# A PEER feed-forward in one block: first products moved behind and between other work, one-hot rows on two engines

## The reference

```python
q = (hf @ w_q).reshape(T, PEER_HEADS, 2, PEER_HALF)
sc = jnp.einsum('thpd,hpkd->thpk', q, subkeys)
s1, i1 = lax.top_k(sc[:, :, 0], 16)
s2, i2 = lax.top_k(sc[:, :, 1], 16)
cand = s1[..., :, None] + s2[..., None, :]          # 16 x 16 pairs
top_s, pos = lax.top_k(cand, 16)                    # the 16 best of them
idx = i1 * 128 + i2 of these; gate = softmax(top_s)
act = gelu(einsum('chkd,cd->chk', u[idx], h))
out = einsum('chk,chkd->cd', gate * act, v[idx])
```

## Time and profile before

| | us |
|---|---|
| median of 3 runs | 3452.93 (3451.11 to 3649.39) |
| profiled execution, span | 3467.7 |
| norm of the feed-forward begins | 2036.7 |
| list of 155 steps | 2193.8 to 2904.3 |
| second products on TensorE | 2932.4 to 3458.8 |

### The profile page before, as it was taken

One profiled execution on the slowest core, in us unless ns is written; L12 is line 12 of the kernel. 1 busy time (PEld: TensorE's weight loads), 2 busy tenths in 40 slices (PEclk: granted clock), 3 DMA queues, 4 the chain that ended last, 5 costly groups with the idle time before them and its releaser, 6 DMA issues. The chain is left out here.

```text
span 3467.7 us, 33649 instructions
## 1 busy us (share of the span) xinstructions
PE 3066.9 (88%) x12681; PEld 2229.5 (64%) x12681; DVE 1723.3 (50%) x3505; ACT 1076.1 (31%) x1596; POOL 488.8 (14%) x357
## 2 busy tenths in 40 slices
PE   7887999699999598778979879698898986999998
PEld 3445666444444244564746568698898986888887
DVE  2255422200000205543442328787879797788886
ACT  2133421100000126674421222234434443333332
POOL 0000000111111000000000000003314143344442
PEclk9995999699999798889779989899999998999999
DMA  3110061488888210021002211357859688999996
GB/s 142 44 50 25 1 145 64 194 329 309 313 315 309 85 49 37 25 97 44 1 26 102 83 55 61 123 193 246 324 178 336 233 305 292 342 369 374 368 374 238
DMA packets 159776, 624.04 MB, mean 180 GB/s; under 512 B 12161, under 2 KB 84481, under 8 KB 128257
## 3 DMA queue, kind: packets, MB, share of 16 engines
q1 hardware_dynamic: 90496, 319.87, 26.1%
q0 software_dynamic: 50688, 276.85, 21.1%
q10 hardware_dynamic: 18432, 25.17, 2.0%
HBM read 555.76 MB, written 66.09 MB: 179 GB/s over the span
## 5 line engine op out<-in xcount | busy, mean ns | idle before, releaser
L1841 POOL DMA_INDIRECT RG<-in_un,EI x128 | 181.6, 1419 | 1400.0 <-DVE EI L2060 1105.3
L2275 PE MATMUL bank<-VH,GL 128*128 128x512 f32 x768 | 300.2, 391 | 29.9 <-DVE VR0r L2264 29.9
L2277 PE MATMUL bank<-VH,GH 128*128 128x512 f32 x768 | 299.7, 390 | 0.0
L1841 POOL DMA_INDIRECT RG<-in_vn,EI x128 | 216.5, 1691 | 446.7 <-DVE X L1855 429.9
L1133 PE MATMUL bank<-UP,HX 128*128 128x512 f32 x480 | 213.0, 597 | 9.4 <-DVE HX L1087 5.5
L1194 DVE SCALAR_TENSOR_TENSOR HN<-SLU,HR,bank 128x256 f32<-128x256 f32 x44 | 21.1, 481 | 344.2 <-ACT SLU L1168 344.2
L2275 PEld LDWEIGHTS bank<-VH,GL 128*128 128x128 f32 x768 | 144.8, 189 | 60.7 <-issue 30.4
L1855 DVE SCALAR_TENSOR_TENSOR X<-RG,DG,X 128x1024 f32<-128x1024 f32 x128 | 164.1, 1282 | 28.2 <-DMA RG<-in_vn,EI 24.1
L1825 PE MATMUL bank<-HTl,UH1r 128*128 128x384 f32 x512 | 174.5, 341 | 0.0
L1826 PE MATMUL bank<-HTh,UH1r 128*128 128x384 f32 x512 | 174.2, 340 | 0.0
L1825 PE MATMUL bank<-HTl,UH0r 128*128 128x384 f32 x512 | 173.3, 338 | 0.0
(11 more groups left out here) (518 smaller groups left out, 6569.3 us busy)
## 6 DMA issues: line engine op xcount, KB each, us to landing
UR<-in_u SPq DMA_DIRECT2D x64, 1024.0 KB, 5.5
VR<-in_vn SPq DMA_DIRECT2D x32, 2048.0 KB, 9.2
W<-in_weights SPq DMA_DIRECT2D x20, 1536.0 KB, 7.3
W<-in_weights SPq DMA_DIRECT2D x14, 2048.0 KB, 8.2
aspill<-GA ACTq DMA_DIRECT2D x128, 192.0 KB, 2.0
wspill<-VR SPq DMA_DIRECT2D x12, 2048.0 KB, 9.2
WW<-wspill SPq DMA_DIRECT2D x32, 768.0 KB, 13.9
AV<-aspill SPq DMA_DIRECT2D x32, 768.0 KB, 16.0
```

The costliest lines, as they stand in the source:

```text
L1841: e.indirect_dma_start(RG[q % RR], None, d["un" if what == "u" else "vn"][:, :], off).then_inc(*row_in[q % RR].up(16))
L2275: e.matmul(bk, r(gl[:, a, t]), r(vh[:, a, :]), start=g == 0 and a == 0, stop=False)
L2277: i = e.matmul(bk, r(gh[:, a, t]), r(vh[:, a, :]), start=False, stop=g == 31 and a == 3)
```

## The change

All of the feed-forward now stands in one block; the query weights have memory of their own, so that their loads and those of u are issued at the start. The search takes the splits of the first two u tiles along.

Of the 128 first products the list keeps 100: 0.95 in a step of choice (54 in 56 steps), 0.47 in another. Eight follow behind the last outer product, and 20 stand between second products, one behind each odd step of the first 40. 104 of the 256 gathered rows lie in the list, the others beside the second products.

Of four OB rows VectorE makes two. ScalarE makes the other two, each as Abs(iota − key) into AB and then Relu(gate − gate x AB), which is the gate at the key and 0 elsewhere. For that ScalarE writes −key and −gate into IN when it writes IA. The outer product waits for both.

A second step now takes all 1024 columns of two rows a (before: 512 columns of four), so v comes in 64 loads of 1 MB (three buffers) and a in 64 of 384 KB (three buffers). The low part of a lies in AV's own place; GL is gone. The last second step signals per token block, and the output leaves in four parts.

The diff, cut:

```diff
-                    for j in range(4):
-                        t = 4 * n + j
-                        i = e.tensor_scalar(OB[n % 2][:, j, :], cc("iota"), IA[:, 1, t:t + 1], IA[:, 2, t:t + 1], ALU.is_equal, ALU.mult)
-                    i.then_inc(*h_hot.up(1))
...
+            def dve_hot(e, n):
+
...
+                t4 = span(n, 4)
+                e.tensor_tensor(OA[n % 2], cc("iota").unsqueeze(1).to_broadcast([128, 4, 128]), IA[:, 0, t4].unsqueeze(2).to_broadcast([128, 4, 128]), ALU.is_equal)
+                for j in range(2):
+                    t = 4 * n + j
+                    i = e.tensor_scalar(OB[n % 2][:, j, :], cc("iota"), IA[:, 1, t:t + 1], IA[:, 2, t:t + 1], ALU.is_equal, ALU.mult)
+                i.then_inc(*h_hot.up(1))
...
+            def act_hot(e, n):
+
...
+                for j in (2, 3):
+                    t = 4 * n + j
+                    k = as_(e.activation(AB[n % 2][:, j - 2, :], cc("iota"), ACT.Abs, bias=IN[:, 0, t:t + 1]))
+                e.wait_ge(as_.sem, k)
+                for j in (2, 3):
+                    t = 4 * n + j
+                    i = e.activation(OB[n % 2][:, j, :], AB[n % 2][:, j - 2, :], ACT.Relu, bias=IA[:, 2, t:t + 1], scale=IN[:, 1, t:t + 1])
+                i.then_inc(*h_act.up(1))
+
+            def pe_outer(e, n):
+                e.wait_ge(*h_hot(n + 1))
+                e.wait_ge(*h_act(n + 1))
...
+            def load_a(e, n):
+                for q in (2 * n, 2 * n + 1):
+                    e.wait_ge(*ga_done[q % 4](16 * (q // 4) + 16))
+                if n >= 3:
+                    e.wait_ge(*y_mm(n - 2))
+                e.dma_start(AV[n % 3][0], AD[n // 2][:, 2 * (n % 2):2 * (n % 2) + 2, :]).then_inc(*a_in[n % 3].up(16))
...
+            def load_v(e, n):
+                if n >= 3:
+                    e.wait_ge(*y_mm(n - 2))
+                e.dma_start(VR[n % 3][0], d["vn"].rearrange("(p g a) n -> g p a n", p=128, g=64)[n]).then_inc(*v_in[n % 3].up(16))
...
+                e.wait_ge(*a_in[n % 3](16 * (n // 3) + 16))
+                a4 = AV[n % 3][0].rearrange("p a (c t) -> p a c t", c=NC)
+                w4 = WW[g % 2].rearrange("p a n -> p (a n)").rearrange("p (c a t) -> p a c t", c=NC, a=4)[:, o:o + 2]
+                e.tensor_tensor(a4, a4, w4, ALU.mult).then_inc(*g_prod.up(1))
...
+                    e.wait_ge(*y_mm(n - 1))
+                e.wait_ge(*g_prod(n + 1))
+                e.activation(r(GH[n % 2]), AV[n % 3][0], ACT.Copy).then_inc(*g_hi.up(1))
...
+                e.wait_ge(*v_in[n % 3](16 * (n // 3) + 16))
+                if n >= 2:
+                    e.wait_ge(*y_mm(n - 1))
+                e.activation(r(VH[n % 2]), VR[n % 3][0], ACT.Copy).then_inc(*v_hi.up(1))
...
+            def pe_second(e, n):
+
+                gh, gl, vh, vl = GH[n % 2], AV[n % 3][1], VH[n % 2], VR[n % 3][1]
+                e.wait_ge(*v_lo(n + 1))
+                e.wait_ge(*g_lo(n + 1))
...
+                for tb in range(3):
+                    t = span(tb)
+                    for half_ in range(2):
+                        c, bk = span(half_, 512), bank[2 + 2 * tb + half_]
+                        for a in range(2):
+                            first, last = n == 0 and a == 0, n == 63 and a == 1
+                            e.matmul(bk, r(gl[:, a, t]), r(vh[:, a, c]), start=first, stop=False)
+                            e.matmul(bk, r(gh[:, a, t]), r(vl[:, a, c]), start=False, stop=False)
+                            i = e.matmul(bk, r(gh[:, a, t]), r(vh[:, a, c]), start=False, stop=last)
...
+            BRIDGE, BESIDE, ROWS1 = 8, 20, 104
+            NM = 14 + 3 * 47
+            choosing = [step < 14 or (step - 14) % 47 < 14 for step in range(NM)]
+            shares = [0.95 if x else 0.0 for x in choosing]
+            rest = (128 - BRIDGE - BESIDE - sum(shares)) / (NM - 56)
+            pace = np.cumsum([x if x else rest for x in shares])
+            firsts = lambda step: range(0 if step == 0 else round(pace[step - 1]), round(pace[step]))
+            NA = 128 - BRIDGE - BESIDE
...
+            def beside(n):
+
+                if n < 0:
+                    return range(NA, NA + BRIDGE)
+                done = lambda m: NA + BRIDGE + min(BESIDE, (m * BESIDE) // 40)
+                return range(done(n), done(n + 1))
...
+                @block.sync
+                def _(e):
+                    e.dma_start(HR3, d["grow"]).then_inc(*g_in.up(16))
+                    for h in range(3):
+                        load_query(e, h)
+                    for n in range(3):
+                        load_u(e, n)
+                    for h in range(3, 8):
+                        load_query(e, h)
...
+                    for n in range(2):
+                        e.wait_ge(*ws_done[n](16 * NC // 2))
+                    e.wait_ge(*o_mm(96))
+                    for n in range(64):
+                        if n % 2 == 0:
+                            load_w(e, n // 2)
+                        load_a(e, n)
+                        load_v(e, n)
+                        if n >= 2:
+                            for q in beside(n - 3):
+                                if q % 2 == 0 and q // 2 + 3 < 64:
+                                    load_u(e, q // 2 + 3)
+                    e.wait_ge(*r_used(256))
+                    e.dma_start(out[span(3), :], X[:, 3, :]).then_inc(out_done.sem, 16)
...
-                        t, bk = span(tb), bank[2 * tb + n % 2]
-                        for a in range(4):
-                            e.matmul(bk, r(gl[:, a, t]), r(vh[:, a, :]), start=g == 0 and a == 0, stop=False)
-                            e.matmul(bk, r(gh[:, a, t]), r(vl[:, a, :]), start=False, stop=False)
-                            i = e.matmul(bk, r(gh[:, a, t]), r(vh[:, a, :]), start=False, stop=g == 31 and a == 3)
...
-                        for n in range(2):
-                            e.wait_ge(*y_mm(63 + n))
-                            for tb in range(3):
-                                o = X[:, tb, span(n, 512)]
-                                e.tensor_tensor(o, o, bank[2 * tb + n], ALU.add).then_inc(*y_add.up(1))
+                        e.wait_ge(*y_add(2 * tb + 2))
+                        e.dma_start(out[span(tb), :], X[:, tb, :]).then_inc(out_done.sem, 16)
+                    e.wait_ge(out_done.sem, 64)
...
+                    for step in range(NM):
+                        for q in firsts(step):
+                            pe_first(e, q)
+                        choice, _, o = matrix(step)
+                        if choice:
+                            pe_chosen(e, *choice)
+                        if o is not None:
+                            pe_outer(e, o)
+                    for q in beside(-1):
+                        pe_first(e, q)
+                    for n in range(64):
+                        pe_second(e, n)
+                        for q in beside(n):
+                            pe_first(e, q)
...
+                        choice, h, o = matrix(step)
+                        if choice:
+                            act_chosen(e, *choice)
+                        if h is not None:
+                            act_hot(e, h)
+                        if o is not None:
+                            act_outer(e, o)
+                        for q in rows(step - 2) if step >= 2 else ():
+                            act_row(e, q)
...
+                    for q in beside(-1):
+                        if q % 2 == 0 and q // 2 + 1 < 64:
+                            act_u(e, q // 2 + 1)
+                        act_first(e, q)
+                    act_v(e, 0)
+                    act_gate(e, 0)
+                    for n in range(64):
+                        if n < 63:
+                            act_v(e, n + 1)
+                            act_gate(e, n + 1)
+                        for q in beside(n):
+                            if q % 2 == 0 and q // 2 + 1 < 64:
+                                act_u(e, q // 2 + 1)
+                            act_first(e, q)
+                        for q in later(n):
+                            act_row(e, q)
...
+                    for q in beside(-1):
+                        if q % 2 == 0 and q // 2 + 1 < 64:
+                            dve_u(e, q // 2 + 1)
+                    dve_v(e, 0)
+                    dve_prod(e, 0)
+                    dve_prod(e, 1)
+                    dve_gate(e, 0)
+                    for n in range(64):
+                        if n < 63:
+                            dve_v(e, n + 1)
+                            if n < 62:
+                                dve_prod(e, n + 2)
+                            dve_gate(e, n + 1)
+                        for q in beside(n):
+                            if q % 2 == 0 and q // 2 + 1 < 64:
+                                dve_u(e, q // 2 + 1)
+                        for q in later(n):
+                            dve_row(e, q)
```

(39 more changed lines are left out.)

731 lines of the change are left out of this document (312 added, 419 removed).

## The result

The changed kernel takes 3604.85 us (median of 4 runs, 3596.21 to 3636.45), the kernel before beside it on the same chip 3464.89: ratio 1.043, 95% interval 1.039 to 1.048. It is 4.3% slower. Some executions of a kernel take a few per cent longer at a lower granted clock (the 3649.39 of the kernel before is one); the medians here hold them, the ratios and intervals, here and in the experiments, leave them out. The forecast was 3490 with a range up to 3545, so both the forecast and the range were wrong. The profiled execution spans 3601.0 us against 3467.7, 133.3 more.

What follows compares the result with a forecast made beforehand. TensorE was taken to bound key choice and second products, VectorE the one-hot phases. Terms −8.6, −67.4, +12.9, +13.2, +91.2 and −4.4 sum to +36.9 on 3452.9, giving 3490 us, range 3400 to 3545.

Steps and rivals of the forecast that it cites:

- Start and key choices: Before and between one-hot phases: earlier query products, −8.6 us; fewer first products per choice step, −67.4 us.
- One-hot phases: Three outer-product phases: ScalarE's rows make a chain and the clock drops in holes; 425 us against 412.1, +12.9.
- both cycles: One-hot phases: 7.9 us through ScalarE's rows, 8.9 with a split of u and VectorE's rows; mean 8.4.
- rival 1: One-hot phases: ScalarE's rows are hidden, no chain binds; phases 329 us, 96 less, total 3394; chance 0.18.
- That sign: One-hot phases: TensorE waits for OB written by ScalarE, not VectorE, 45 waits or more of 1.5 to 3 us.
- The hole of 1.8 us: One-hot phases: TensorE idles 1.8 us between the earlier outer product's end and the one awaiting ScalarE's rows.
- Rival 5: One-hot phases: Abs and Relu between Gelu reload ScalarE's table, 96 times two loads; given no chance.
- Pause: Boundary before second products: 8 first products fill 33.3 us, then 8.0 us idle; 41.3 against 28.1, +13.2.
- Second products: Last stage: 20 first products at 4.16 us add 83.2, transfers and late AV tiles 8; sum +91.2 us.
- Rival 2: Second products: transfers bind, AV lands over 6.4 us after issue and delays the gate split; +44, 3534; chance 0.12.
- bounds under "wrong if": Forecast wrong if the three one-hot phases total under 370 us, or second products exceed 640 (transfers).
- Tail: End of kernel: three of four output blocks leave early, adds start earlier; 8.9 to 4.5 us, −4.4.

Runs made afterwards that it cites:

- e3: e1 with ScalarE's one-hot rows of a step put ahead of its split of u and its Gelu; 3533.12 us, ratio 1.021 to the kernel before.
- e9: e8 with no first products beside the second ones: 20 back in the list, 8 behind the last outer product; 3373.85 us, ratio 0.971 to the kernel before.
- e1: The changed kernel with SyncE issuing the u loads of the last 28 first products where their wait is already over; 3509.19 us, ratio 1.014 to the kernel before.
- e8: e5 plus e6's order of gate split before gate product, and all tiles of the last part placed alike; 3414.46 us, ratio 0.985 to the kernel before.
- e6: e4 with VectorE's gate split ahead of the next gate product, and v's and the query's tiles 1920 bytes on; 3443.68 us, ratio 0.995.
- e7: e4 with no first products beside the second ones, and a change of bank after 3 matmuls, not 6; 3437.76 us, ratio 0.991 to the kernel before.
- e4: e1 with all four one-hot rows on VectorE and none on ScalarE; 3462.88 us, ratio 1.001 to the kernel before.
- e5: e3 with VectorE's one-hot rows also ahead of its split of u, and v's tiles 32 bytes on; 3445.99 us, ratio 0.996 to the kernel before.
- e2: e1 with the area of AV, WW, GH, OA and OB placed 32 bytes higher; 3517.58 us, ratio 1.015 to the kernel before.

## Why the prediction was right or wrong

**Start and key choices: right.** The first two choices take 111.8 us (112 forecast), the other two 113.5 (119); TensorE is busy there for 54.9 of 58.0 and 54.9 of 58.5. Start and first choices together came to −48.3 and not −51.5.

**One-hot phases: right in sum and in both cycles, wrong in blaming one of them alone.** 420.2 against 425. The prices held: Abs 386 ns and Relu 486 against the 0.39 and 0.48 named (groups from 2299.8 to 2833.4: count, busy, mean ns).

```profile
L2098 ACT ACTIVATE OB<-C,IA,IN 128x128 f32<-128x128 f32 x192 | 84.4, 486 | 3.2
L2094 ACT ACTIVATE C<-C,IN 128x128 f32<-128x128 f32 x192 | 64.8, 386 | 19.0 <-PE bank L2107 18.0 <-ACT GA L1957 0.9
```

The granted clock of 0.91, 0.93 and 0.94 makes 61 us at the low level, 56 were forecast. From GA's start to the end of the rows there are 2.5 us, as worked out. The prediction named both cycles, 7.9 us through ScalarE's rows and 8.9 through the split and VectorE's rows, but its words and rival 1 made ScalarE's rows the one cause; e3 showed that taking away only that half lengthens the other. Rival 1 (rows hidden, 329) came near only with both orders turned (353). The waits were to name ScalarE; the profile names VectorE's OB, 42 times. That sign was badly chosen rather than missing: by the rows themselves ScalarE's are the later ones in 29 holes and VectorE's in 22 (experiment 3). The hole of 1.8 us named for a cycle without a split is there (1.74). Rival 5 gave nothing: there are 8 table loads behind 2190 us, and 9 in before.

**Pause: mechanism right, a load left out.** +25.8, not +13.2. The 8.0 us from the start of the last GA are there (2880.40 to 2888.4, and in e9 the pause is 41.2 against 41.3 forecast). What was left out is that tile 53 of u, for the seventh of the eight bridge products, stands in SyncE's list behind the waits for the WS stores and for `ga_done` and behind eight loads (start, duration):

```profile
2854.97 0.44 SPq L2133 DMA_DIRECT2D VR<-in_vn  x1
2855.45 25.27 SPq L1929 DMA_DIRECT2D UR<-in_u  x4
...
2865.53 1.91 ACT L1935 ACTIVATE UH1r<-UR 128x2048 fp32r<-128x2048 f32 x1 [14.96 <-DMA UR<-in_u]
```

That is SyncE's and ScalarE's timeline of the changed kernel; TensorE's wait for it in the pause (total, times, longest):

```profile
PE bank L1948 <- DVE UR2r L1939: 11.4, 1, 11.4
```

**Second products: the step that failed.** It reads "in the first 40 steps u and GA add 1 us but TensorE adds 2.1, so there is room". That balanced the bytes; it didn't walk SyncE's list, in which the loads of AV and v stand behind a load of u that waits for its buffer. Taking that wait out of their way gave back 71.0 us (e1). Of the term's 182.0 us:

| part | us | from |
|---|---|---|
| 20 first products | 83 | forecast; steps of 12.6 against 8.4 |
| `load_u`'s wait ahead of AV and VR | 71.0 | after − e1 |
| pitch 0.2333, not 0.2267, 2304 times | 15.4 | trace; e8 has 0.2267 again |
| VectorE's product ahead of the gate split, and transfers | 12.6 | the rest; e6 took 18.5 with the order alone |

Taking the 20 first products out gave 77 us (e7, e9) and not 83; with 77 the rest is 18.6. The 15.4 us of the pitch have no place in the prediction either: it took the matmuls of a second step to stand as close as before ("TensorE's own count stays"). It also sets the transfers' 8.39 us against 8.13 of TensorE where the earlier trace rows gives 8.22, which makes 4 us of its 6.

The prediction called that last order free while AV lands within 6.4 us. With the loads of u out of the way (e4) VectorE still waited 24.6 us for AV and TensorE 11.0 us behind it. The text had 8 us for this and the transfers, too little by 5 to 11. Rival 2 had the shape (late AV behind VectorE's order) but blamed the queue's rate and priced it at 44; the share of 0.73, and 0.96 in e9, shows that there was rate left. The second of the bounds under "wrong if" (over 640) was met, with the reason in brackets (transfers) wrong.

**Tail: right**, −4.6 against −4.4.

That moving 20 first products to where TensorE binds costs their full 4.16 us was the likeliest part of the sum and nearly held: a step with one is 4.1 to 4.2 us longer than one without, and 3.8 to 3.9 each come back when they go (e7, e9), against 1.6 to 2.3 in the phases.

## What to carry to other kernels

Walk the list of an engine that issues loads instruction by instruction, with the time at which each one's wait is met; one early prefetch with a far wait delays every load behind it, and no count of bytes shows it. Where rows or small operands are shared out to a second engine, put them ahead of the long work on both engines, or the helper makes the chain longer. Where an instruction waits for two engines and the profile names one, match it with its own operands before believing the name. Put extra TensorE work where TensorE has holes: the same first product cost 1.6 us there and 3.8 beside work that fills it.

## What the runs showed of the hardware

In these kernels the spacing of 512-column products in fp32r goes with where their two operands lie. The remainders of the tiles' starts in 512 bytes, worked out from the sizes allocated ahead of them, and the spacing in us (median over the 384 query products; for the second ones the median over six in a row, as in experiment 8):

| kernel | HTh, HTl | query's QH, QW | v | GH, AV | query | second |
|---|---|---|---|---|---|---|
| before | 96 | 96 | 96 | 96 | 0.227 | 0.2267 |
| after | 96 | 224 | 224 | 256 | 0.232 | 0.2333 |
| e5 | 96 | 256 | 256 | 288 | 0.232 | 0.2333 |
| e6 | 96 | 96 | 96 | 128 | 0.227 | 0.2333 |
| e8 | 96 | 96 | 96 | 96 | 0.227 | 0.2267 |

Query products take HTh or HTl as the moving and QH or QW as the stationary tile, second ones v and GH or AV. With equal remainders they stand 5 to 7 ns closer together; each kernel fits, e2 too (224 and 288, 0.2333). The Trainium skill (TensorE: Matmul & The Clock Gate, Step-by-step: what each phase is for) says that loading the next weights takes no SBUF read bandwidth from the running matmul. These runs don't show which read is held up, if one is; they do show that the placement of the two operands costs 3%. Whether 96 itself, the equality, or another distance than 512 bytes decides is open: no other placements were run.
